# Activations of the dense expert half kept in SBUF, eight gather buffers late in the fetched half

## What is computed

```python
def peer_ffn(h, w_q, keys, u_tab, v_tab):      # 16384 experts, tables of 16384 x 1024 f32
    ...
    q = (xc @ w_q).reshape(PEER_BLOCK, PEER_HEADS, 2, PEER_KEY_DIM // 2)
    s = jnp.einsum("chsd,hskd->chsk", q, keys)             # 8 heads, 2 sides, 128 keys
    top_s, top_i = lax.top_k(s, PEER_TOPK)                 # 16 of each side
    cand = top_s[:, :, 0, :, None] + top_s[:, :, 1, None, :]
    best_s, best = lax.top_k(cand.reshape(...), PEER_TOPK) # 16 of the sums
    e = i1 * PEER_NKEYS + i2                               # the expert's number
    g = jax.nn.softmax(best_s, axis=-1)
    act = jax.nn.gelu(jnp.einsum("cd,chkd->chk", xc, u_tab[e]))
    return jnp.einsum("chk,chkd->cd", g * act, v_tab[e])
```

## Time and profile before

| | |
|---|---|
| median of 3 runs | 3607.93 us (3606.14 to 3617.26) |
| the profiled execution | 3610.36 us, span 3608.4 us |
| PE busy | 2761.9 us, 77% of the span |
| DVE busy | 2299.1 us, 64% |
| POOL busy | 1232.2 us, 34% |
| ACT busy | 597.0 us, 17% |
| mean granted PE clock | 0.877 of full speed |
| moved by DMA | 984.8 MB, mean 273 GB/s |

### The profile page before, as it was taken

How to read it: one execution, slowest core, us unless ns; L and a number is a source line. 1 busy time by engine, 2 the same in 40 slices (tenths; PEclk the granted TensorE clock), 3 DMA queues, 4 the chain that set the end, 5 groups by cost and what they waited for, 6 DMA issues and landing times. The chain is left out here.

```text
span 3608.4 us, 36802 instructions
## 1 busy us (share of the span) xinstructions
PE 2761.9 (77%) x13254; PEld 2273.7 (63%) x13254; DVE 2299.1 (64%) x4452; ACT 597.0 (17%) x964; POOL 1232.2 (34%) x1092
## 2 busy tenths in 40 slices
PE   8968897898999999996001977888999999996000
PEld 7744466777888888885000756777888888885000
DVE  6635527898775556655666147898774556655666
ACT  6543413112121000000002423112121000000000
POOL 0000000043344455545663000043344455545663
PEclk9977798998999999998555988999999999998555
DMA  9610013398999999999884213398999999999885
GB/s 362 246 65 27 3 44 111 118 356 286 327 348 409 412 409 406 395 380 345 273 275 164 76 59 111 134 343 290 333 346 387 409 409 409 394 368 349 272 274 192
DMA packets 286594, 984.83 MB, mean 273 GB/s; under 512 B 30144, under 2 KB 63840, under 8 KB 278880
## 3 DMA queue, kind: packets, MB, share of 16 engines
q0 software_dynamic: 156672, 570.49, 43.1%
q1 hardware_dynamic: 94944, 378.66, 28.1%
q10 hardware_dynamic: 34816, 33.56, 2.6%
HBM read 942.76 MB, written 39.85 MB: 272 GB/s over the span
## 5 line engine op out<-in xcount | busy, mean ns | idle before, releaser
L1144 POOL DMA_INDIRECT all_xT<-in_u_rows,peer_eidx x512 | 596.0, 1164 | 1847.7 <-DVE peer_eidx L1329 1094.3
L1409 DVE SCALAR_TENSOR_TENSOR peer_hs<-all_xT,peer_dots,peer_hs 128x1024 f32<-128x1024 f32 x508 | 653.0, 1285 | 405.7 <-DMA all_xT<-in_peer_v,peer_eidx 390.3
L1402 DVE CUSTOM_DVE_ANT_0 all_xT<-all_xT,peer_hs 128x1024 f32<-128x1024 f32 x512 | 622.2, 1222 | 347.7 <-DMA all_xT<-in_u_rows,peer_eidx 338.6
L1144 POOL DMA_INDIRECT all_xT<-in_peer_v,peer_eidx x512 | 598.8, 1170 | 487.0 <-DVE peer_hs L1409 415.9
L1162 PE MATMUL exp_out<-peer_hd,all_ring 128*128 128x256 f32 x2752 | 623.8, 383 | 29.0 <-SPq L1122 20.1
L1189 PE MATMUL exp_down<-peer_gates,all_ring 128*128 128x256 f32 x2720 | 611.5, 381 | 12.8 <-DMA all_ring<-in_peer_v 12.2
L1162 PEld LDWEIGHTS exp_out<-peer_hd,all_ring 128*128 128x128 f32 x2752 | 519.3, 191 | 108.5 <-SPq L1122 20.5
L1189 PEld LDWEIGHTS exp_down<-peer_gates,all_ring 128*128 128x128 f32 x2720 | 510.4, 190 | 103.5 <-DMA all_ring<-in_peer_v 36.1
L1207 PE MATMUL exp_ps_t<-all_ident,peer_hs 128*128 128x128 f32 x16 | 3.9, 428 | 485.6 <-DVE peer_hs L1409 485.6
L1162 PE MATMUL exp_out<-peer_hd,spare_ring 128*128 128x256 f32 x1344 | 315.7, 389 | 39.1 <-ACT spare_acts L1217 32.2
L1189 PE MATMUL exp_down<-peer_gates,spare_ring 128*128 128x256 f32 x1376 | 314.6, 382 | 8.3 <-DMA spare_ring<-in_peer_v 8.1
(11 more groups left out here) (258 smaller groups left out, 3203.6 us busy)
## 6 DMA issues: line engine op xcount, KB each, us to landing
all_ring<-in_uT SPq DMA_DIRECT2D x172, 512.0 KB
all_ring<-in_peer_v SPq DMA_DIRECT2D x170, 512.0 KB
ada_raw<-in_ada_tiles SPq DMA_DIRECT2D x48, 1024.0 KB, 5.2
spare_ring<-in_peer_v SPq DMA_DIRECT2D x86, 512.0 KB
spare_ring<-in_uT SPq DMA_DIRECT2D x84, 512.0 KB
activations<-spare_acts ACTq DMA_DIRECT2D x128, 256.0 KB
spare_hin<-activations POOLq DMA_DIRECT2D x64, 512.0 KB
all_ring<-in_w_peer_q SPq DMA_DIRECT2D x22, 512.0 KB
```

Source lines behind the costliest of these rows:

```text
L1144: nc.gpsimd.indirect_dma_start(out=rows[n % 4], out_offset=None, in_=table, in_offset=bass.IndirectOffsetOnAxis(ap=q.eidx[:, b, k:k + 1], ...
L1402: nc.vector.tensor_tensor_reduce(out=row, in0=row, in1=own[:, b, :], scale=1.0, scalar=0.0, op0=ALU.mult, op1=ALU.add, accum_out=q.dots[:, ...
L1409: nc.vector.scalar_tensor_tensor(out=acc[:, b, :], in0=row, scalar=q.dots[:, b, k:k + 1], in1=acc[:, b, :], op0=ALU.mult, op1=ALU.add).the ...
```

## The change

The activations are no longer stored to DRAM. A table says after which pair of chunks PE and ACT do each group of gates, and so, for each pair of chunks and each token, which comes first, the activation or the gate:

- The activation comes first: ACT writes the gelu straight into the gates' place. When the gates of that group are in PSUM, DVE multiplies them onto these activations (`spread`), and ACT copies the gates only for the keys whose activation is still to come.
- The gate comes first: ACT writes the gelu into one of four small buffers `acts`, and DVE multiplies it onto the gates (`post`).

A pair may be cut between the two, by tokens. Because activations are written into `gates` from the first chunk on, what lay in its second half must go: `kept` and `idx` move to the first half, the routing tiles move behind key 82 (`first_late`), ACT waits with chunk 82 until routing is over (`routed`), `pick` moves elsewhere and has one side instead of two, and routing has 23 steps where it had 17 (steps 10 to 15 are done for one side after the other). All tables are drawn out: one-hots stand at every sixth slot (30 to 120 and 126 to 216; before, every third, 21 to 66 and 76 to 121), and routing of block 1 ends at slot 121, its softmax at 123. The second pass waits once, for all gates, spreads and posts.

From slot 248 on, rows go to eight buffers: four more (`far`) lie over the one-hot matrices, which are done by then.

```diff
+        PAIRS = NKEYS // 2
+        NEAR = 248
+        GATES_AFTER = {13 + 9 * g // 5: g for g in range(GROUPS)}
+        GATES_AFTER.update({41 + 7 * g // 5: GROUPS + g for g in range(GROUPS)})
+        DONE_AFTER = {g: 2 * p + 2 for p, g in GATES_AFTER.items()}
...
+        ROUTE_AT.update({32 + 21 * n // 10: (3, n) for n in range(STEPS)})
+        ROUTE_AT.update({82 + 18 * n // 10: (1, n) for n in range(STEPS)})
+        SOFTMAX_AT = {5: 0, 23: 2, 80: 3, 123: 1}
+        COLUMNS_AT = {28: 2, 124: 3}
+        HOTS_AT = {30 + 6 * g: g for g in range(GROUPS)}
+        HOTS_AT.update({126 + 6 * g: GROUPS + g for g in range(GROUPS)})
+        SPREAD_AT = {39 + 6 * g: g for g in range(GROUPS)}
+        SPREAD_AT.update({135 + 6 * g: GROUPS + g for g in range(GROUPS)})
+        POST = [p for p in range(PAIRS) if p > min(GATES_AFTER)]
+        POST_AT = {41 + 342 * (p - 14) // 100 if p <= 40 else 130 + 4 * (p - 40): p for p in POST}
+
+        def known(p):
+            n = P // TG * DB * TG
+            for after, g in GATES_AFTER.items():
+                if after >= p:
+                    n = min(n, g * TG)
+            return min(n, P), max(n - P, 0)
...
-                if n >= 4:
+                if n >= NEAR + 8:
+                    pool.wait_ge(s_used, n - 7)
+                elif n >= NEAR + 4:
+                    pool.wait_ge(s_gmm, DB * GROUPS)
+                elif n >= 4:
                     pool.wait_ge(s_used, n - 3)
...
-                if n in LOAD_H_AT:
-                    g = LOAD_H_AT[n]
-                    for j in range(2):
-                        pool.wait_ge(s_hst[j], 16 * (g + 1))
-                    if g >= 2:
-                        pool.wait_ge(s_w, g - 1)
-                    pool.dma_start(q.hin[g % 2][:, :, :, :], h_dram[g]).then_inc(s_hin[g % 2], 16)
...
                 if g >= 2:
                     pe.wait_ge(s_gev, g - 1)
+                    pe.wait_ge(s_spread, g - 1)
...
-                if c % 4 == 0:
-                    pe.wait_ge(s_w, c // 4 + 1)
...
             pe.wait_ge(s_gev, DB * GROUPS)
+            pe.wait_ge(s_spread, DB * GROUPS)
+            pe.wait_ge(s_post, len(POST))
...
-                if c % 2 == 0 and pair >= 2:
-                    act.wait_ge(s_hst[pair % 2], 16 * (pair // 2))
...
+                if p in POST and c % 2 == 0 and p - 4 in POST:
+                    act.wait_ge(s_post, POST.index(p - 4) + 1)
+                if c == q.first_late:
+                    act.wait_ge(s_routed, 1)
+                from_ = outs[:, c % 2, 0:DENSE].rearrange("p (b n) -> p b n", b=DB)
+                if post == (0, 0):
+                    last = act.activation(gates[:, :, c, :], from_, ACT.Gelu_apprx_tanh)
+                elif post == (P, P):
+                    last = act.activation(held[:, :, c % 2, :], from_, ACT.Gelu_apprx_tanh)
+                else:
+                    for b, n in enumerate(post):
+                        if n > 0:
+                            last = act.activation(held[:, b, c % 2, 0:n], from_[:, b, 0:n], ACT.Gelu_apprx_tanh)
+                        if n < P:
+                            last = act.activation(gates[:, b, c, n:P], from_[:, b, n:P], ACT.Gelu_apprx_tanh)
+                last.then_inc(s_act, 1)
...
+            def spread(g):
+                b, k, c = g // GROUPS, g % GROUPS, DONE_AFTER[g]
+                dve.wait_ge(s_gev, g + 1)
+                dve.wait_ge(s_act, c)
+                cut = gates[:, b, 0:c, k * TG:(k + 1) * TG]
+                nc.vector.tensor_tensor(cut, cut, ps_g[g % 2][:, :, 0:c].rearrange("p k n -> p n k"),
+                                        ALU.mult).then_inc(s_spread, 1)
+
+            def post(p):
+                dve.wait_ge(s_act, 2 * p + 2)
+                dve.wait_ge(s_gev, sum(after < p for after in GATES_AFTER))
+                held, (n0, n1), pair = q.acts[p % 4], known(p), slice(2 * p, 2 * p + 2)
+                if n1 == P:
+                    cut = gates[:, :, pair, :].rearrange("p b c n -> p b (c n)")
+                    last = nc.vector.tensor_tensor(cut, cut, held[:, :, :, :].rearrange("p b c n -> p b (c n)"), ALU.mult)
+                else:
+                    cut = gates[:, 0, pair, 0:n0]
+                    last = nc.vector.tensor_tensor(cut, cut, held[:, 0, :, 0:n0], ALU.mult)
+                    if n1 > 0:
+                        cut = gates[:, 1, pair, 0:n1]
+                        last = nc.vector.tensor_tensor(cut, cut, held[:, 1, :, 0:n1], ALU.mult)
+                last.then_inc(s_post, 1)
```

More of the change, by code:

```diff
@@ L925, in __init__ @@
         self.place = tops.sb("place", [P, 2, HK], BF16)
[L926 to L927 removed]
+        self.less = tops.sb("less", [P, 2, PH, TOPK])
         self.den = tops.sb("den", [P, 2, PH])
[L929 removed]
+        self.pack = tops.sb("pack", [P, NB - FETCHED, 3, HK])
+        self.pair = tops.sb("pair", [P, 2, HK])
         self.rest = tops.sb("rest", [P, 2, P])
         spare = Lay(nc, f"spare{l}", split_at, 2 * KD * SEQ * 4)
+        self.far = [nc.alloc_sbuf_tensor_at(f"far{l}_{j}", [P, D], F32, offset=split_at + j * D * 4) for j in range(4)]
         self.hot = [spare.sb(f"hot{j}", [P, 4, TG // 2, NKEYS, 2], BF16) for j in range(2)]
[L934 to L935 removed]
+        self.acts = [spare.sb(f"acts{j}", [P, 2, 2, P]) for j in range(4)]
         self.ring = spare.sb("ring", [P, KD, P])
+        self.pick = spare.sb("pick", [P, PH, TOPK, TOPK], BF16)
 def query_phase(nc, t, l, xT, x_dram, hi, lo, ring, hs, ident, q):
@@ L1097, in experts_phase, with row_of, turn_of @@
         rows = [xT[:, 2 * j:2 * j + 2, :].rearrange("p k n -> p (k n)") for j in range(4)]
+        rows += [x[:, :] for x in q.far]
+        def row_of(n):
+            return n % 4 if n < NEAR else n % 8
+        def turn_of(n):
+            return n // 4 if n < NEAR else (n - NEAR) // 8 + (NEAR // 4 if n % 8 < 4 else 0)
         own = hs[:, :, :].rearrange("p k n -> p (k n)").rearrange("p (b d) -> p b d", b=FETCHED)
@@ L1107, in experts_phase @@
         s_in = [r.sem(f"in{j}") for j in range(R)]
-        s_row = [r.sem(f"row_in{j}") for j in range(4)]
-        s_hst = [r.sem(f"acts_stored{j}") for j in range(2)]
-        s_hin = [r.sem(f"acts_back{j}") for j in range(2)]
+        s_row = [r.sem(f"row_in{j}") for j in range(8)]
         s_back = r.sem("stream_back")
@@ L1212, in gelu @@
             def gelu(c):
-                pair = c // 2
+                p = c // 2
+                post = known(p)
+                held = q.acts[p % 4]
                 act.wait_ge(s_mm, c + 1)
-                if c % 2 == 0 and pair >= 2:
-                    act.wait_ge(s_hst[pair % 2], 16 * (pair // 2))
-                act.activation(q.acts[pair % 2][:, :, c % 2, :],
-                               outs[:, c % 2, 0:DENSE].rearrange("p (b n) -> p b n", b=DB),
-                               ACT.Gelu_apprx_tanh).then_inc(s_act, 1)
@@ L1231, in _ @@
             for c in range(NKEYS):
                 gelu(c)
-                if c in EXP_AFTER:
-                    b = EXP_AFTER[c]
+                if c % 2 == 1 and c // 2 in EXP_AFTER:
+                    b = EXP_AFTER[c // 2]
+                    slot_of = q.less[:, ORDER.index(b) % 2, :, :]
                     act.wait_ge(s_less, ORDER.index(b) + 1)
-                    act.activation(q.less[:, b, :, :], q.less[:, b, :, :], ACT.Exp).then_inc(s_exp, 1)
-                if c in GATES_AFTER:
-                    take_gates(GATES_AFTER[c])
+                    act.activation(slot_of, slot_of, ACT.Exp).then_inc(s_exp, 1)
@@ L1239, in _ @@
+                if c % 2 == 1 and c // 2 in GATES_AFTER:
+                    take_gates(GATES_AFTER[c // 2])
             for b in range(FETCHED):
@@ L1421, in _ @@
                     columns(COLUMNS_AT[i])
+                if i == max(COLUMNS_AT):
+                    settled()
+                    dve.sem_inc(s_routed, 1)
+                if i in SPREAD_AT:
+                    spread(SPREAD_AT[i])
                 if i in HOTS_AT:
                     one_hots(HOTS_AT[i])
-                if i in WEIGHT_AT:
-                    weigh(WEIGHT_AT[i])
+                if i in POST_AT:
+                    post(POST_AT[i])
             dve.wait_ge(s_used, SLOTS)
```

115 lines of the change are left out of this document (50 added, 65 removed).

## The result

The changed kernel takes 3344.55 us (median of 4 runs, 3335.79 to 3352.21), the kernel before 3607.03 (4 runs, 3588.74 to 3617.26). The ratio is 0.9277, 95% interval 0.9231 to 0.9322. The forecast was 3354. The profiled execution took 3349.14 us, span 3347.4.

The account below looks back on a forecast made before the run. The fetched half's 512 slots, one after the other, were taken to bound the kernel. Layer end moves from 1945 to 1818, 127 us; 3610.4 less 2 x 127 gives 3356, against the median 3354; its own range 3300 to 3410 (chance 0.59).

Parts of the forecast that it names:

- The bound: Each layer: 512 slots of the fetched half, one after the other, end it; what can be won is time per slot.
- The first half: Slots 0 to 225: 2.45 us a slot, slot 225 at 1266, PE's second pass from 1270 to 1731.
- surcharge: DVE's products with strided PSUM reads: no extra cost taken, with 1.5 times (13 us more) as the bound.
- Beside the second pass: From 1334 to 1731, with eight buffers: 264 GB/s for rows, 1.99 us a slot, 199 slots in 397 us.
- The tail: After PE's second pass: the 57 slots left take 87 us, the layer ends at 1818 against 1945.
- POOL's 1.52 binds: In the tail: POOL's 1.22 us plus 0.30 us between issues sets the pace, above DVE's 1.35 us.
- Layer 1: Second layer: has the same tail, so gets the same gain as layer 0, 127 us.
- 1: Whole smoother than assumed: first half at 2.29 us a slot, layer end 1774, 171 us a layer, 3266 us; chance 0.12.
- 2: Eight buffers bring little beside the stream: traffic stays at 381 GB/s, 2.22 us a slot, 3414 or 3478 us; chance 0.15.
- 3: Gathers starve PE's weights beside the stream: PE gets 64 GB/s and ends the layer at 1950, 3618 us; chance 0.05.
- 4: Handshakes of DVE, ACT and PE hold the first half at 2.93 us a slot: layer end 1926, 3570 us; chance 0.08.
- 5: Deep queues lower total traffic to 356 GB/s: 2.48 us a slot, 68 us a layer, 3472 us; chance 0.01.

Follow-up runs that it names:

- experiment 5: Changed kernel with one of the three one-hot products of a group, which PE multiplies three times (gates not the reference's): 3292.65 us.
- experiment 6: Changed kernel with a fifth row buffer from slot 128, in the place of pick (nine buffers from slot 248): 3287.87 us, ratio 0.911.
- experiment 1: Changed kernel without the switch to eight buffers, four to the end: 3499.54 us, ratio 0.971.
- experiment 2: Kernel before with eight buffers from slot 248, activations still through DRAM: 3434.26 us, ratio 0.9529.
- experiment 3: Kernel of experiment 2 with eight buffers from slot 128 instead of 248: 3422.48 us, ratio 0.95.
- experiment 4: Changed kernel with the activations' traffic put back as dummy stores after each pair of chunks and dummy loads after slot 240: 3467.34 us, ratio 0.9621.
- experiment 9: Changed kernel whose last 64 slots of a layer add only 256 of the 1024 columns (sums not the reference's): 3335.12 us.

## Why the prediction was right

**The bound.** That the fetched half ends each layer, and that what can be won is time per slot, held before and after: PE waits 73 us for the last row.

**The first half.** Slot 225 was forecast at 1266 and PE's second pass at 1270; they came at 1274 and 1275. The rate was 2.49 us and not 2.45. The working priced spreads at 26 us and posts at 24. In the trace they are 24.7 (31 of the 32, up to 1272) and 24.0, of which the last two lines hold 23.3:

```profile
L1422 DVE TENSOR_TENSOR peer_gates<-peer_gates,exp_down 128x224 f32<-128x224 f32 (+30 forms) x31 | 24.7, 796 | 0.0
...
L1434 DVE TENSOR_TENSOR peer_gates<-peer_gates,spare_acts 128x256 f32<-128x256 f32 (+15 forms) x49 | 17.0, 347 | 9.3 <-ACT peer_gates L1252 9.3
...
L1437 DVE TENSOR_TENSOR peer_gates<-peer_gates,spare_acts 128x48 f32<-128x48 f32 (+14 forms) x21 | 6.3, 299 | 0.0
```

So this product carries no surcharge for its strided read from PSUM. That DVE's work and the gathers are nearly level and neither hides the other is what experiments 5 and 6 show, from both sides. That the choice of 2.45 between 2.29 and 2.93 came out so close is partly luck, for nothing in the rows of before fixed it. Two of the smaller readings were off and changed nothing: the first 128 slots before took 371 us, 2.90 us each and not 2.93, and by the tables ACT writes 48 pairs cut by tokens, in three pieces a chunk, where the working has 28 pairs and up to four pieces. Its waits for PE covered that: PE waited for no gelu up to 1275.

**Beside the second pass.** 1.99 us a slot was forecast, 2.00 measured, at 410 GB/s; experiments 1 to 4 show both parts of that step, the ceiling and that four buffers don't reach it. The second pass took 472 us and not 461. PE waited 14.7 us for weights instead of 9.2, and its first 16 products took 6.5 us, where they took 3.7 in the kernel before. PE had stood idle for 10.9 us just ahead of them, where it came from the first pass with 0.2 us between in the kernel before, and the granted clock was 0.59 on average while they ran, near the lower of its two levels (1.2 of 2.4 GHz):

```profile
1275.00:1282.00 7.00, 6.91 (x19) 5.66 (x20) 4.64 (x7) 0.00 (x0) 5.36 (x4) 0.59 0.84 255
1282.00:1290.00 8.00, 8.00 (x38) 6.79 (x38) 3.80 (x8) 0.00 (x0) 4.01 (x4) 1.00 0.90 317
```

These two account for 8 of the 11 us; the rest is open.

**The tail.** "POOL's 1.52 binds": POOL does, at 1.39. The term was mis-sized because the mean of 1.216 us mixed 74 gathers of 0.94 us with 60 longer ones, of up to 1.93; in the steady tail of the changed kernel they take 1.08 to 1.09. Over 51 slots that is 7 us a layer, and it made up for the 7 us by which slot 256 was late (1341 for 1334). So the end comes out closer than the terms: 1818 forecast, 1821 measured; 127 us gained in layer 0 forecast, 124 measured.

**Layer 1.** It was given the same gain on the strength of its tail. But its 512 slots took 1242 us before, where those of layer 0 took 1233, and 1107 us after (2207.1 to 3313.8), where those of layer 0 took 1110. It gained 135 us and not 127, which is why the medians are 262 us apart where 254 were forecast.

**The rivals.** 1 did not come: 2.49 us is above its 2.29. 2 is refuted by 410 GB/s beside the stream, 3 by PE's 14.7 us of waits for weights in the whole pass with eight rows under way, 4 by the 2.49 us a slot, against its 2.93, and DVE's 9.3 us of waits for other engines up to 1272, and 5 by the slices of 409 in each layer.

## What to carry to other kernels

Price saved traffic by the stretch in which it runs: the same 16.8 MB cost 6 to 11 us where the total was below the ceiling, and 50 us where it was at it. For a loop that is held by gathers, read a rate per slot for every stretch. Ask of each stretch whether it is at the ceiling of the traffic, at an engine's own time, or at the round trip of its buffers; in these runs only stretches in which the last had a part got faster with more buffers, and memory that other tiles had finished with was the place for them. Where work is spread over such a loop by a table, try drawing it in: here the table that let PE's second pass begin 40 us sooner won 36 us in all, together with the earlier switch of buffers.

## What the runs showed of the hardware

- One core moved 409 to 412 GB/s for up to 400 us at a stretch with rows and weights, or rows, weights and activations, under way. In experiment 9 it moved as much with the queue of 4 KB rows alone, for some 60 us (404 in its window, 410 by the steady 1.28 us a slot).
- The length of a gather's issue on POOL went with what DVE did: 0.94 us while DVE ran short sums (experiment 9), 1.08 beside back-to-back sums of 1.28 us.
- While the dummy loads of experiment 4 ran, the total reached 400 GB/s and not 409. The number of kinds of traffic is not the reason, for the kernel before had rows, weights and activation loads at 409; what is, no run here separates.
- After 10.9 us without work, PE's first products of the second pass ran at a granted clock of 0.59 (1275 to 1282), and the next at 1.00.
